# Encoder layer on one core: the distance table moved ahead of the input, and two half-norms interleaved in one row of steps

## The chip, the cores and the metric

The kernel runs on one core of a Trainium2 chip. The metric is device time in microseconds (us) of one launch; lower is better. The core's engines are TensorE (PE), VectorE (DVE), ScalarE (ACT), GpSimd (POOL) and SyncE (SP, which issues most of the DMAs). Each engine works through its own queue in order; semaphores tie the queues together.

## The reference, cut to what matters

One layer of a hybrid attention encoder over 512 prompt tokens and 64 sample tokens, all in float32:

```python
u = rms_norm(h, g_mix_pre)                       # h: 576 tokens x 1024
qa, ka, va, qb, kb, vb = split(u @ w_in)
lam = exp(sum(lq[0]*lq[1])) - exp(sum(lq[2]*lq[3])) + lam0
oa  = band_attention(qa, ka, va, rel_bias)       # mixer A, 8 heads of 64
s   = qb @ kb.T / 8 - slope[head] * abs(q_pos - k_pos)      # mixer B, ALiBi distance penalty
ob  = rms_norm((softmax(s0) - lam * softmax(s1)) @ vb) * (1 - lam0)
g_a, g_b = sigmoid(u @ w_gate)
mix = (g_a * (oa @ w_branch_a) + g_b * (ob @ w_branch_b)) @ w_out
h = h + rms_norm(mix, g_mix_post)                                       # update 0
f = square(relu(rms_norm(h, g_ffn_pre) @ w_up)) @ w_down
h = h + rms_norm(f, g_ffn_post)                                         # update 1
h = h + sigmoid(h @ w_ple_gate) * rms_norm(p @ w_ple, g_ple)
```

## The kernel before, in words

Activations lie transposed (128 channels of a block k on the partitions, 576 tokens along the free axis); a block k is one of KB = 8. Every large product is made in float32 precision from three passes: weights and activations are split into a high and a low part, and TensorE adds hi*hi, lo*hi and hi*lo. A weight piece of 128x512 is loaded by SP into `w_raw`, its high part is made by ScalarE (`hi_part`, L757), its low part by GpSimd (`lo_part`, L569), and TensorE multiplies it. Tokens are taken in two halves of 288 (h = 0, 1).

**The start.** SP loads x (`x_tm`, L428 to L434). TensorE turns it (L1791), ScalarE makes `act_hi` (`split_x`, L770), VectorE makes `act_lo` and keeps `hT` (L1181, L1184). The first of these need `gcol`, the gains, which VectorE copies at L1176. TensorE then makes the k, q and v of unit 0 (L1816, L1736). VectorE scales them by the row of norms (`projected`: k at L1216, q at L1213, v at L1216 once more, as `projected(Count(0), 2)`, L1249). Between q and v stand, in VectorE's queue: the two lambda products and their sum (L1231 to L1234), the distance table (L1236 to L1244: it waits for GpSimd's iota at L590, casts it to float, takes the absolute value, overwrites a corner and halves it into `tab_b[0]`), a wait for ScalarE's exponential of the lambda sums, and two instructions on it (L1246, L1248). TensorE's next work after the v product is to turn v (`V4`, L1894), so it waits for L1216. Then it computes the first scores (`S 0`, L1859) and three steps of unit 1's projection (L1736, 18 matmuls) before the next scores. GpSimd halves the table for the next head at L654, behind its weight splits.

**The updates.** After the output product, and again after the last down product, the layer adds a normalised block sum to `hT`. This is `update(n, ...)`, n = 0 or 1, in VectorE's queue, with partners of the same step order in three other queues. For each block k and half h:

- `normed_half(k, h)` (L1459) multiplies the block by gain and norm row, which TensorE has put into `score` (`half_row`, L2039, announced by `row_ready`). For k in 2, 5, 7 VectorE also adds the block to `hT` (L1464); for the others GpSimd does (L716).
- ScalarE (`split_hi`, L961 or L963, then L965) makes `act_hi` of the new block and puts a copy of the block into the one PSUM place `h_stage`. It refills `h_stage` only when VectorE has read the one before.
- `rest(k, h)` (L1470 for n = 0, L1475 for n = 1) makes `act_lo` from `h_stage` and posts `h_split`.
- TensorE (`behind_norm`, L2076, products at L2048) multiplies two output blocks by block k of half h when `h_split` says so, first all k of half 0, then all of half 1.

VectorE runs `normed_half` two blocks ahead of `rest` within a half: all of half 0 with its eight rests, then a wait for the second `row_ready`, then half 1, which begins with three `normed_half` and the add of block 2 before its first rest.

Of the kernel before, what the change touches and what calls it, by code (L numbers as in the profile page):

```python
# [28 lines left out]
ALU, ACT, AX = mybir.AluOpType, mybir.ActivationFunctionType, mybir.AxisListType  # L29
# [4 lines left out]
MASK = -1e30  # L34
# [68 lines left out]
def at_least(eng, sem, count):  # L103

    v = count.value()
    assert not count.terms or count.const > 0
    if not isinstance(v, int) or v > 0:
        eng.wait_ge(sem, v)
# [9 lines left out]
def encoder_layer(nc, x_prompt, x_sample, cache_a_k, cache_a_v, cache_b_k, cache_b_v, p_prompt, p_sample,  # L118
# [4 lines left out]
    SMP = x_sample.shape[1]  # L123
# [3 lines left out]
    KB = D // P  # L127
# [7 lines left out]
    TW = SEQ + P  # L135
# [37 lines left out]
    CHAIN = (0, 2, 3, 5)  # L173
# [12 lines left out]
    with ExitStack() as ctx:  # L186
        def sb(name, shape, dt=F32, stack=ctx):
            return stack.enter_context(nc.sbuf_tensor(name, shape, dt))

        def sem(name):  # L190
            return ctx.enter_context(nc.semaphore(name))
# [26 lines left out]
        with ExitStack() as band_only:  # L218
            sb("oa_hi_first", [P, T], F32, band_only)
            tab_b = [sb(f"tab_b{b}", [P, TW], F32, band_only) for b in range(2)]  # L220
# [3 lines left out]
        with ExitStack() as branch_a:  # L224
            oa_hi, oa_lo = sb("oa_hi", [P, NA, T], F32R, branch_a), sb("oa_lo", [P, NA, T], F32R, branch_a)

            with ExitStack() as att:
# [12 lines left out]
                with ExitStack() as early:  # L240
                    dist_i, dist = sb("dist_i", [P, TW], I32, early), sb("dist", [P, TW], F32, early)
# [87 lines left out]
        consts, dist_made = sem("consts"), sem("dist_made")  # L329
# [10 lines left out]
        tab_ready = sem("tab_ready")  # L340
# [19 lines left out]
        row_ready, row_read = sem("row_ready"), sem("row_read")  # L360
# [21 lines left out]
        def tokens(h):  # L382
            return slice(HALF * h, HALF * h + HALF)

        def last_square(n, k, h):

            return SQUARES[n] + KB - 2 + 2 * h + k - (KB - 2)
# [753 lines left out]
        def _(dve):  # L1141
            own = [Count(0)]

            def done(ins):

                ins.then_inc(vec, 1)
                own[0] = own[0] + 1

            def settle():

                at_least(dve, vec, own[0])
# [17 lines left out]
            for b in range(2):  # L1169
# [2 lines left out]
                dve.memset(o_tm[b][SMP:P, QB - 1], 0.0)  # L1172
                dve.memset(o_ms[SMP:P, b, QB - 1:QB], 0.0)

            dve.wait_ge(rows_turned, 1)
            dve.tensor_copy(gcol[:, 0:8], proj[0][:, 0:8]).then_inc(gains_ready, 1)  # L1176

            for i, (j, h) in enumerate(X_TILES):
# [3 lines left out]
                                         in1=act_hi[:, j, c].bitcast(F32), op0=ALU.mult, op1=ALU.subtract  # L1182
# [44 lines left out]
            for n in range(2):  # L1227
# [5 lines left out]
            settle()  # L1233
            dve.tensor_reduce(lam_s[:, 0:2], lam_pr[:, :, :], AX.X, ALU.add).then_inc(lam_ready, 1)  # L1234

            dve.wait_ge(dist_made, 1)  # L1236
            done(dve.tensor_copy(dist[:, :], dist_i[:, :]))
            settle()
            done(dve.scalar_tensor_tensor(out=tab_b[0][:, :], in0=dist[:, :], scalar=-1.0, in1=dist[:, :],
                                          op0=ALU.mult, op1=ALU.max))  # L1240
            settle()
            done(dve.memset(tab_b[0][0:SMP, TW - SMP:TW], -2e2 * MASK))
            settle()
            dve.tensor_scalar(tab_b[0][:, :], tab_b[0][:, :], -0.5, None, ALU.mult).then_inc(tab_ready, 1)  # L1244
            dve.wait_ge(lam_exped, 1)
            done(dve.tensor_tensor(lam_s[:, 0:1], lam_s[:, 3:4], lam_s[:, 2:3], ALU.subtract))  # L1246
            settle()
# [165 lines left out]
            with dve.Fori(0, KB // 2) as it:  # L1413
                for j in range(2):
                    n = Count(j, [(it, 2)])
# [10 lines left out]
            def add_square(n, first=False, cols=slice(0, T)):  # L1426

                dve.wait_ge(squared, n + 1)
                if first:
                    dve.tensor_copy(sq_sum[:, cols], sq[n % 2][:, cols]).then_inc(sq_added, 1)  # L1430
                else:
                    dve.wait_ge(sq_added, n)
                    dve.tensor_tensor(sq_sum[:, cols], sq_sum[:, cols], sq[n % 2][:, cols], ALU.add
                                      ).then_inc(sq_added, 1)
# [7 lines left out]
            def means(n, h):  # L1442

                dve.wait_ge(sum_turned, CHAIN[n] + h + 1)
                c = slice(3 * h, 3 * h + 3)
                dve.tensor_scalar(ms_t[0:THIRD, c], turn[0:THIRD, c], 1.0 / D, EPS, ALU.mult, ALU.add
                                  ).then_inc(ms_ready, 1)
# [6 lines left out]
            def update(n, x, g, keep):  # L1454


                def normed_half(k, h):
                    c = tokens(h)
                    dve.scalar_tensor_tensor(out=x[:, k, c], in0=x[:, k, c], scalar=gcol[:, g + k:g + k + 1],  # L1459
                                             in1=score[:, 512 * h:512 * h + HALF], op0=ALU.mult, op1=ALU.mult  # L1460
                                             ).then_inc(block_normed, 1)
                    if k in BY_VECTOR:
                        dve.wait_ge(block_normed, (2 * n + h) * KB + k + 1)
                        dve.tensor_tensor(hT[:, k, c], hT[:, k, c], x[:, k, c], ALU.add).then_inc(h_added[1], 1)  # L1464

                def rest(k, h):
                    c = tokens(h)
                    dve.wait_ge(h_hi, (2 * n + h) * KB + k + 1)
                    if n == 0:
                        dve.scalar_tensor_tensor(out=act_lo[:, k, c], in0=h_stage,  # L1470
                                                 scalar=gcol[:, G_FPRE + k:G_FPRE + k + 1],
                                                 in1=act_hi[:, k, c].bitcast(F32), op0=ALU.mult, op1=ALU.subtract
                                                     ).then_inc(h_split, 1)
                    else:
                        dve.tensor_tensor(act_lo[:, k, c], h_stage, act_hi[:, k, c].bitcast(F32), ALU.subtract  # L1475
                                          ).then_inc(h_split, 1)

                for k in range(KB - 2, KB):
                    keep(k, 0)
                for k in range(KB - 2, KB):  # L1480
                    add_square(last_square(2 * n, k, 0), cols=tokens(0))
                means(2 * n, 0)
                keep(KB - 2, 1)
                add_square(last_square(2 * n, KB - 2, 1), cols=tokens(1))
                dve.wait_ge(row_ready, CHAIN[2 * n] + 1)
                normed_half(0, 0)
                normed_half(1, 0)
                keep(KB - 1, 1)
                add_square(last_square(2 * n, KB - 1, 1), cols=tokens(1))
                for k in range(2, KB):  # L1490
                    normed_half(k, 0)
                    rest(k - 2, 0)
                    if k == 2:
                        means(2 * n, 1)
                rest(KB - 2, 0)
                rest(KB - 1, 0)
                dve.wait_ge(row_ready, CHAIN[2 * n] + 2)
                for k in range(KB):
                    normed_half(k, 1)
                    if k >= 2:  # L1500
                        rest(k - 2, 1)
                rest(KB - 2, 1)
                rest(KB - 1, 1)

            for m in range(KB - 2):
                b = (PJ_OUT + m) % 2
# [723 lines left out]
```

## Time and profile before

| what | value |
|---|---|
| three runs | 1117.22, 1113.8, 1116.96 us; median 1116.96 us |
| the profiled execution's own time | 1117.23 us |
| its span in the trace | 1115.6 us |
| TensorE busy | 1091.6 us (98%) |
| VectorE, ScalarE, GpSimd busy | 52%, 47%, 47% |
| mean granted TensorE clock | 0.994 of full |

The profiled execution has 1.6 us outside its span. Shares are averages over the whole span. The granted clock has two levels, 1.0 (2.4 GHz) and 0.5 (1.2 GHz).

### The profile page before, as it was taken

To read this page: it belongs to the slowest core of one execution; us is meant where nothing else is said; L and a number is where in the kernel's file an instruction comes from. 1 tells how busy PE (TensorE), PEld (TensorE's weight loads), DVE (VectorE), ACT (ScalarE), POOL (GpSimd) and SP (SyncE) were. 2 spreads that over 40 slices of the span, in tenths; PEclk is the share of its full clock that TensorE was granted. 3 is DMA by queue.
4 is the path that set the end of the run, shared out by engine and by line. 5 is a ranking of instruction groups with operands and counts; after the bars stand their busy time and mean duration, and the time that the engine had idled before them with its cause. 6 is when DMAs were issued, how large, how long until landed. Compare 5 with 4: busy or idle time off the path is not lost.

```text
span 1115.6 us, 22618 instructions
## 1 busy us (share of the span) xinstructions
PE 1091.6 (98%) x8252; PEld 1049.1 (94%) x8252; DVE 583.7 (52%) x1192; ACT 521.3 (47%) x1119; POOL 526.7 (47%) x432
## 2 busy tenths in 40 slices
PE   8899999999999999999999999999999999999897
PEld 7899999999889889999999989999999999999897
DVE  5656766666656641112442564878316613833755
ACT  6355455555555553331233467346424722743652
POOL 3556555565455424343445544454444444443651
PEclk9899999999999999999999999999999999999999
DMA  8234434343243322232222213232322322322123
GB/s 185 67 88 105 106 93 100 100 117 88 61 105 98 98 70 85 81 100 79 81 85 79 73 53 90 80 86 82 104 85 77 115 76 75 105 86 76 57 77 85
DMA packets 219618, 99.14 MB, mean 89 GB/s; under 512 B 62786, under 2 KB 216635, under 8 KB 219539
## 3 DMA queue, kind: packets, MB, share of 16 engines
q1 hardware_dynamic: 214098, 88.74, 29.8%
q0 software_dynamic: 5440, 9.34, 2.6%
q8 instruction: 50, 0.82, 0.3%
q14 instruction: 30, 0.24, 0.1%
HBM read 88.57 MB, written 11.02 MB: 89 GB/s over the span
## 4 chain that ended last, share of the span: by engine, by line
PE 90%; DVE 5%; ACT 2%; issue 1%; DMA 1%; SPq 0%; ACTq 0%; DVEq 0%
PE proj L1736 62%; PE proj L2135 12%; PE score L1859 3%; PE proj L2048 2%; PE turn_out L1919 2%; PE turn_out L1949 2%; PE turn_out L1941 1%; PE turn_out L1946 1%; PE score L1871 1%; PE proj L2009 1%; DMA x_tm<-x_sample 1%; PE turn_out L1894 1%; ACT turn_out L965 1%; DVE hT L1464 0%; DVE act_lo L1470 0%
## 5 line engine op out<-in xcount | busy, mean ns | idle before, releaser
L569 POOL TENSOR_TENSOR w_lo<-w_raw,w_hi 128x512 fp32r<-128x512 f32 x292 | 389.7, 1341 | 468.8 <-ACT w_hi L757 468.2
L757 ACT ACTIVATE w_hi<-w_raw 128x512 fp32r<-128x512 f32 x292 | 181.8, 628 | 303.2 <-PE proj L1736 259.6
L1736 PE MATMUL proj<-act_hi,w_hi 128*128 128x288 f32 x1088 | 246.5, 308 | 0.7 <-ACT wide L1124 0.3
L1736 PE MATMUL proj<-act_lo,w_hi 128*128 128x288 f32 x1088 | 233.6, 296 | 0.0
L1736 PE MATMUL proj<-act_hi,w_lo 128*128 128x288 f32 x1088 | 233.1, 296 | 0.0
L1736 PEld LDWEIGHTS proj<-act_hi,w_hi 128*128 128x128 f32 x1088 | 172.6, 190 | 12.5 <-issue 7.4
L1736 PEld LDWEIGHTS proj<-act_hi,w_lo 128*128 128x128 f32 x1088 | 175.6, 189 | 0.0
L1736 PEld LDWEIGHTS proj<-act_lo,w_hi 128*128 128x128 f32 x1088 | 175.4, 189 | 0.0
L1736 PE MATMUL proj<-mid_hi,w_hi 128*128 128x288 f32 x608 | 130.5, 295 | 0.0
L1736 PE MATMUL proj<-mid_lo,w_hi 128*128 128x288 f32 x608 | 130.4, 295 | 0.0
L1736 PE MATMUL proj<-mid_hi,w_lo 128*128 128x288 f32 x608 | 130.3, 295 | 0.0
L1736 PEld LDWEIGHTS proj<-mid_hi,w_hi 128*128 128x128 f32 x608 | 97.5, 188 | 0.0
L1736 PEld LDWEIGHTS proj<-mid_hi,w_lo 128*128 128x128 f32 x608 | 97.4, 188 | 0.0
L1736 PEld LDWEIGHTS proj<-mid_lo,w_hi 128*128 128x128 f32 x608 | 97.3, 188 | 0.0
L820 ACT ACTIVATE prob<-prob,neg_max 128x128 f32<-128x128 f32 (+4 forms) x108 | 62.5, 580 | 66.1 <-DVE neg_max L1265 65.8
L1265 DVE CUSTOM_DVE_ANT_0 prob<-score,tab_b 128x128 f32<-128x128 f32 (+4 forms) x80 | 40.9, 539 | 35.8 <-PE score L1859 19.4
L1559 DVE TENSOR_TENSOR wide<-proj,wide 128x576 f32<-128x576 f32 x24 | 18.1, 754 | 73.7 <-PE proj L1736 73.7
L846 ACT ACTIVATE probT<-turn_out 128x512 f32<-128x512 f32 (+3 forms) x88 | 38.0, 431 | 36.5 <-PE turn_out L1919 22.9
L1384 DVE TENSOR_TENSOR wide<-proj,x_row 128x576 f32 (+1 forms) x13 | 9.9, 758 | 73.9 <-PE proj L1736 73.9
L1919 PE MATMUL turn_out<-ident,prob 128*128 128x128 f32 x208 | 36.3, 278 | 0.5 <-DVE mid_lo L1365 0.4
L2048 PE MATMUL proj<-act_hi,w_hi 128*128 128x288 f32 x96 | 30.9, 322 | 4.9 <-DVE act_lo L1475 2.1
L1265 DVE CUSTOM_DVE_ANT_0 prob<-score,tab_a 128x128 f32<-128x128 f32 (+4 forms) x40 | 20.4, 541 | 18.5 <-PE score L1859 13.4
(312 smaller groups left out, 2106.9 us busy)
## 6 DMA issues: line engine op xcount, KB each, us to landing
w_raw<-w_in SPq DMA_DIRECT2D x72, 256.0 KB, 3.3
w_raw<-w_up SPq DMA_DIRECT2D x64, 256.0 KB, 2.9
w_raw<-w_down SPq DMA_DIRECT2D x64, 256.0 KB, 2.8
w_raw<-w_gate SPq DMA_DIRECT2D x32, 256.0 KB, 2.8
w_raw<-w_branch_b SPq DMA_DIRECT2D x16, 256.0 KB, 2.7
w_raw<-w_out SPq DMA_DIRECT2D x16, 256.0 KB, 2.8
w_raw<-w_ple_gate SPq DMA_DIRECT2D x16, 256.0 KB, 2.8
out<-k_out SPq DMA_DIRECT2D x48, 64.0 KB, 1.9
```

The costliest lines, as they stand in the source:

```text
L569: pool.tensor_tensor(w_lo[:, slot], w_raw[:, slot], w_hi[:, slot].bitcast(F32), ALU.subtract).then_inc(lo_done, 1)
L757: act.activation(w_hi[:, slot], w_raw[:, slot], ACT.Copy).then_inc(hi_done, 1)
L820: act.activation(prob[b][m][0:np_, 0:n], prob[b][m][0:np_, 0:n], ACT.Exp, scale=-1.0, bias=neg_max[0:np_, b, m:m + 1], accum_out=sums[0:np ...
L846: act.activation(probT[m][0:np_, 0:n], turn[0:np_, 0:n], ACT.Copy).then_inc(turn_free, 1)
L1265: last = dve.tensor_tensor_reduce(prob[b][m][rs, 0:n], score[rs, 512 * m:512 * m + n], tab, -1.0, 3e38, ALU.add, ALU.min, neg_max[rs, b, m ...
L1559: dve.tensor_tensor(halves(d), acc[b], halves(d), ALU.add).then_inc(proj_free[b], 1)
L1736: last = pe.matmul(out[:, h], w[:, slot, at], x[:, k, HALF * h:HALF * h + HALF], start=(k == 0 and s == 0), stop=(k == blocks - 1 and s == 2))
L1859: last = pe.matmul(score[:, 512 * m:512 * m + n], q[par][h, P * i:P * i + P], k[par][h, 0:n], start=(s == 0), stop=(s == 2))
L1919: last = pe.transpose(turn[:, P * j:P * j + P], prob[i % 2][0 if i == QB - 1 else m][:, P * j:P * j + P], ident[:, :])
L1949: last = pe.matmul(outp[:, 0:P], probT[0][:, P * j:P * j + P], v_tm[:, j, :], start=(j == 0), stop=(j == i))
L2048: last = pe.matmul(acc[n % 2][:, h], w[:, slot, at], x[:, k, tokens(h)], start=(k == 0 and s == 0), stop=(k == KB - 1 and s == 2))
L2135: last = pe.matmul(bank, a[:, at], b[:, k0 + k, cols], start=(k == 0 and s == 0), stop=(k == KB // 2 - 1 and s == 2))
```

## The change

Two edits, both in VectorE's queue. The number and kind of instructions stay the same. The four instructions of the distance table and their wait go from behind the lambda sums to behind the first memsets, ahead of the copy of the gains. In `update`, the two loops over half 0 and half 1 become one loop of 16 steps in which `normed_half` runs two steps ahead of `rest` across the border of the halves, with the wait for the second norm row ahead of step 8.

```diff
                 dve.memset(o_ms[SMP:P, b, QB - 1:QB], 0.0)
 
+            dve.wait_ge(dist_made, 1)
+            done(dve.tensor_copy(dist[:, :], dist_i[:, :]))
+            settle()
+            done(dve.scalar_tensor_tensor(out=tab_b[0][:, :], in0=dist[:, :], scalar=-1.0, in1=dist[:, :],
+                                          op0=ALU.mult, op1=ALU.max))
+            settle()
+            done(dve.memset(tab_b[0][0:SMP, TW - SMP:TW], -2e2 * MASK))
+            settle()
+            dve.tensor_scalar(tab_b[0][:, :], tab_b[0][:, :], -0.5, None, ALU.mult).then_inc(tab_ready, 1)
+
             dve.wait_ge(rows_turned, 1)
             dve.tensor_copy(gcol[:, 0:8], proj[0][:, 0:8]).then_inc(gains_ready, 1)
...
             dve.tensor_reduce(lam_s[:, 0:2], lam_pr[:, :, :], AX.X, ALU.add).then_inc(lam_ready, 1)
 
-            dve.wait_ge(dist_made, 1)
-            done(dve.tensor_copy(dist[:, :], dist_i[:, :]))
...
-            dve.tensor_scalar(tab_b[0][:, :], tab_b[0][:, :], -0.5, None, ALU.mult).then_inc(tab_ready, 1)
             dve.wait_ge(lam_exped, 1)
...
-                for k in range(2, KB):
-                    normed_half(k, 0)
-                    rest(k - 2, 0)
-                    if k == 2:
+                for step in range(2, 2 * KB + 2):
+                    if step == KB:
+                        dve.wait_ge(row_ready, CHAIN[2 * n] + 2)
+                    if step < 2 * KB:
+                        normed_half(step % KB, step // KB)
+                    rest((step - 2) % KB, (step - 2) // KB)
+                    if step == 2:
                         means(2 * n, 1)
-                rest(KB - 2, 0)
-                rest(KB - 1, 0)
-                dve.wait_ge(row_ready, CHAIN[2 * n] + 2)
-                for k in range(KB):
-                    normed_half(k, 1)
-                    if k >= 2:
-                        rest(k - 2, 1)
-                rest(KB - 2, 1)
-                rest(KB - 1, 1)
```

## Rows read from the trace of the kernel before

**Rows 1.** The page: chain that ended last, shares by engine.

```profile
PE 90%; DVE 5%; ACT 2%; issue 1%; DMA 1%; SPq 0%; ACTq 0%; DVEq 0%
```

**Rows 2.** Waits of PE: line waited for: total us, times, longest.

```profile
PE turn_out L1894 <- DVE vT L1216: 2.8, 1, 2.8
```

**Rows 3.** Timeline of VectorE, 34 to 42 us: start, length, what [idle before].

```profile
34.59 1.42 DVE L1237 CAST dist<-dist_i 128x640 f32<-128x640 int32 x1
36.05 1.80 DVE L1239 SCALAR_TENSOR_TENSOR tab_b<-dist 128x640 f32<-128x640 f32 x1
...
39.26 1.21 DVE L1246 TENSOR_TENSOR lam_s<-lam_s 128x1 f32<-128x1 f32 x1
...
40.58 0.75 DVE L1216 TENSOR_TENSOR vT<-proj,x_row 128x576 f32<-128x576 f32 x1
```

**Rows 4.** Timeline of PE: last matmuls ahead of the wait for v.

```profile
38.29 0.43 PE L1736 MATMUL proj<-act_lo,w_hi 128*128 128x288 f32 x2
```

**Rows 5.** Chain in order of time, units 0 and 1: start, length, what.

```profile
41.47 1.09 PE turn_out L1894 x4
42.56 0.83 PE score L1859 x5
43.39 4.62 PE proj L1736 x18
...
73.79 0.59 PE turn_out L1894 x4
74.38 0.48 PE score L1859 x6
74.86 2.57 PE proj L1736 x18
```

**Rows 6.** Windows: busy us by engine, then granted PE clock, DMA share, GB/s.

```profile
45.00:46.00 1.00, 1.00 (x6) 1.00 (x6) 0.96 (x3) 0.00 (x0) 0.00 (x0) 0.50 0.00 0
...
649.00:650.00 1.00, 1.00 (x6) 1.00 (x6) 0.96 (x3) 0.87 (x3) 0.57 (x1) 0.50 0.00 0
```

**Rows 7.** Timeline of GpSimd, 34 to 44 us.

```profile
34.24 1.43 POOL L605 TENSOR_TENSOR q_lo<-q_raw,q_hi 128x576 fp32r<-128x576 f32 x1
35.62 1.54 POOL L569 TENSOR_TENSOR w_lo<-w_raw,w_hi 128x512 fp32r<-128x512 f32 x1
...
41.66 1.82 POOL L654 TENSOR_SCALAR tab_b<-tab_b 128x640 f32<-128x640 f32 x1
```

**Rows 8.** Timeline of the start: GpSimd, VectorE and ScalarE.

```profile
1.42 0.66 POOL L590 IOTA dist_i<- 128x640 int32 x1
...
5.88 0.17 DVE L1176 COPY gcol<-proj 128x8 f32<-128x8 f32 x1 [2.94 <-PE proj L1784]
...
8.65 0.89 ACT L770 ACTIVATE act_hi<-score,gcol 128x288 fp32r<-128x288 f32 x2 [0.59 <-PE score L1791]
```

**Rows 9.** Timeline of VectorE, update 1, border of the halves.

```profile
1050.32 0.46 DVE L1475 TENSOR_TENSOR act_lo<-turn_out,act_hi 128x288 fp32r<-128x288 f32 x1 [0.48 <-ACT turn_out L965]
1051.26 0.46 DVE L1475 TENSOR_TENSOR act_lo<-turn_out,act_hi 128x288 fp32r<-128x288 f32 x1 [0.48 <-ACT turn_out L965]
1051.63 1.36 DVE L1459 SCALAR_TENSOR_TENSOR wide<-wide,gcol,score 128x288 f32<-128x288 f32 x3
1053.02 1.06 DVE L1464 TENSOR_TENSOR hT<-hT,wide 128x288 f32<-128x288 f32 x1
1054.01 0.45 DVE L1475 TENSOR_TENSOR act_lo<-turn_out,act_hi 128x288 fp32r<-128x288 f32 x1
...
1056.79 0.46 DVE L1464 TENSOR_TENSOR hT<-hT,wide 128x288 f32<-128x288 f32 x1
```

**Rows 10.** Timeline of PE: norm row and first product of half 1, both updates.

```profile
647.32 0.41 PE L2048 MATMUL proj<-act_hi,w_hi 128*128 128x288 f32 x1 [1.75 <-DVE act_lo L1470]
...
1043.45 0.80 PE L2039 MATMUL score<-ident,r_t 96*128 96x96 f32 x6
...
1054.51 0.40 PE L2048 MATMUL proj<-act_hi,w_hi 128*128 128x288 f32 x1 [1.68 <-DVE act_lo L1475]
```

**Rows 11.** GpSimd's adds in the updates: count, min/median/max ns, first and last start.

```profile
L716 POOL TENSOR_TENSOR hT<-hT,wide x20: 785/805/810, 628.9 to 1058.1; 128x288 f32<-128x288 f32 x20
```

More of the change, by code:

```diff
@@ L1234, in _ @@
             dve.tensor_reduce(lam_s[:, 0:2], lam_pr[:, :, :], AX.X, ALU.add).then_inc(lam_ready, 1)
-            dve.wait_ge(dist_made, 1)
-            done(dve.tensor_copy(dist[:, :], dist_i[:, :]))
[L1238 to L1243, printed above, removed]
-            dve.tensor_scalar(tab_b[0][:, :], tab_b[0][:, :], -0.5, None, ALU.mult).then_inc(tab_ready, 1)
             dve.wait_ge(lam_exped, 1)
```

## The prediction

> **What bounds the kernel now.** I read the page's chain first: 90% of it is TensorE's own work [rows 1], so the change can only pay where TensorE stands still or runs slowly. The waits of TensorE come next. The longest single one in the list is the turning of the first v, behind VectorE's L1216: 2.8 us, once [rows 2]. Two more of 1.75 and 1.68 us stand where the products of half 1 begin in the two updates [rows 10]. The change touches exactly these three places. The windows add what the list of waits hides: after the first wait TensorE runs at a granted clock of 0.50, the 1.2 GHz level [rows 6].
>
> **Part A, the table, taken off the path.** TensorE's last v matmuls end at 38.29 + 0.43 = 38.72 [rows 4]. L1216 could start then, but starts at 40.58 because VectorE is still in the table (34.59 to about 39.3) and then in L1246, which lasts to 40.47 [rows 3]. Without the table, L1246 is reached at about 34.6 plus ScalarE's small exponential. It is drawn out by GpSimd: the cast beginning at 34.59 ended at 36.01, 0.34 us after GpSimd's q_lo ended at 35.67, and L1239 ended at 37.85, 0.69 after the split that ended at 37.16 [rows 3, 7]. So L1246 may stand until one GpSimd instruction ends (about 36 to 37), still well before 38.72. Then L1216 starts with the end of the matmuls, about 38.76 (the trace's usual hand-over is a few hundredths), lasts 0.75, and TensorE begins 0.14 after its end, as before (41.33 to 41.47) [rows 3, 5]. That is 39.65 instead of 41.47: 1.82 us. What is late next is v itself, so a wait of 0.93 us stays.
>
> **Part A, the clock.** From 41.47, four transposes, the first scores and 18 matmuls take 1.09 + 0.83 + 4.62 = 6.54 us at the lower level [rows 5, 6]. The same three pieces in unit 1, with no wait ahead of them, take 0.59 + 0.48 + 2.57 = 3.64 [rows 5]. What TensorE did before the clock fell was to stand still for 2.75 us (38.72 to 41.47). If the 0.93 us that stay don't bring the clock down, 2.90 us more are saved; if they do, nothing of it. So the term lies between 0 and 2.90. I take 2.90. The nearest rows are the two of about 1.7 us: the one before 647.32 was followed by 0.50 some 1.7 us later, the one before 1054.51 left the matmul behind it at its usual 0.40 [rows 6, 10]. Waits of 1.7 us are thus the borderline of this trace and 0.93 is about half of them.
>
> **Part A, where the table goes.** VectorE is idle from 2.94 to 5.88, waiting for TensorE's turned gains [rows 8]. The iota it needs has ended at 2.08, so the new wait does not hold. Behind it stand only the gain copy and its users; ScalarE first uses the gains at 8.65 [rows 8]. The price of the table with GpSimd in the way is 34.59 to about 39.3, 4.7 us, so it ends at 7.7 at worst, and the copy of 0.17 is done before 8.65. Without GpSimd, which has no arithmetic there, cast and absolute value cost 0.34 and 0.69 plus some hundredths each, and the halving is taken like the cast, one input and as many elements: an estimate of 1.5 to 2 us, inside the 2.94 that are idle. Either way the cost is nothing. If that cover were gone, each further microsecond would shift the whole start.
>
> This placement has one rule against it. The Trainium skill, page "SBUF — State Buffer" (the "DVE blocks DMA" trap), says that VectorE instructions which take both read ports, fp32 copies among them, keep GpSimd from writing the descriptors of DMAs it issues, so that such DMAs starve. By that rule the x loads would suffer if GpSimd issued them; they stand in SP's queue, so by the rule the sum stays as it is. No run here shows a load issued by GpSimd beside such a copy.
>
> **Part A, what comes next.** At full clock the second scores are due at 39.65 + 3.64 = 43.29. They need VectorE's two bias instructions on the first scores, and in the trace these came only when GpSimd's halving (41.66 to 43.48) was over [rows 7]. That halving stands behind four splits which the table held up: by 0.34 and 0.69 for its first two instructions, about 1.4 us in all. It now ends between 42.1 and 43.5. The pair then takes at most 0.9, by two of the normed halves of 0.45 that have over twice as many columns [rows 9]. So it is done between 42.6 (at half of that) and 44.4, and a new wait of 0 to 1.1 us may appear here. I take 0, since most of the 1.4 us should come back.
>
> **Part B, the row of 16.** In update 1 the rests of blocks 6 and 7 of half 0 begin at 1050.32 and 1051.26, each after 0.48 us in which VectorE waits for ScalarE's stage [rows 9]. Only behind them come three normed halves (1051.63, 1.36 for the three), the add of block 2 (1.06, at 1053.02) and the first rest of half 1 at 1054.01; TensorE, which had waited 1.68, goes on at 1054.51 [rows 9, 10]. In the new order the first two normed halves go ahead of those two rests. One costs some 0.45 to 0.5, so each fits the 0.48 in which VectorE stood. The second norm row that they wait for has been there since 1043.45 + 0.80 = 1044.25 [rows 10], over 5 us earlier; nothing queued behind the moved wait is held.
>
> After the rest of block 7 (done 1051.7) there remains one normed half and the add. The add took 1.06 because GpSimd was in its own adds, of 0.8 us each [rows 11]. Now GpSimd gets its first two blocks at about 1050.3 and 1051.2 and is done near 1052.0, so the add of VectorE should take the 0.46 that it takes alone [rows 9]; 1.06 is the upper bound. The sum: 1051.63 + 0.46 for one normed half (1.36/3), + 0.46 for the add = 1052.55 for the first rest, against 1054.01: 1.46 us sooner. ScalarE has the stage filled by then: it must wait for the rest of block 7 at 1051.7, and VectorE never stood longer than 0.48 for it in the rows of that border.
>
> TensorE's half 0 ended 1.68 before 1054.51, at 1052.83; its first product of half 1 then starts at 1053.05. From there half 1 runs at the pace of the rests, as before, since that chain (stage, rest, stage) is unchanged: all eight shift by 1.46, and so does TensorE's end. With the add at 1.06 the gain is 0.86; the upper bound is the whole wait, 1.68. In update 0 the rows repeat 407 us earlier, with the wait of 1.75 before 647.32 [rows 10]; the gain there is again 1.46. The lower clock there (649 to 650) [rows 6] costs nothing now, as the rests and not TensorE's speed set the end of that half; a smaller wait can only make it rarer. Part B: 2 x 1.46 = 2.92, bounds 1.7 to 3.4. Work after both updates is TensorE's own again, so it shifts as a whole.
>
> **Sum.** 1.82 + 2.90 + 2.92 = 7.64 us off the profiled 1117.23 gives 1109.6. That execution lies 0.27 above the median of 1116.96. The run at 1113.8 is 3.4 lower than the other two, near the 2.9 that the low clock costs: some executions of the kernel before may escape it.
>
> **The rivals.**
> - *The clock falls all the same.* The remaining 0.93 us, followed by transposes and small scores, is enough. For it: one 1.75 us wait did bring the clock down. Against: it is half as long. Then 1.82 + 2.92 = 4.74: 1112.5.
> - *The row of 16 pays little.* The add and the stage of half 1 collide with GpSimd and ScalarE, and the first rest comes hardly sooner, since ScalarE's single stage is the real pace. For it: every rest of half 0 waited for ScalarE [rows 9]. Against: between 1051.7 and 1054.0 it was VectorE that was busy throughout. Gain 4.72 from part A alone: 1112.5.
> - *The table does not free v.* L1246 is held behind GpSimd's back-to-back splits up to the point where v would have been late anyway, and the clock falls too. For it: its 1.21 us for one column [rows 3]. Against: four us of slack. With part B only: 1114.3.
> - *Slower: the early table holds up the start.* Place: VectorE from 2.94, ahead of the gain copy. Price: one us for each us by which the copy ends after 8.65, as ScalarE's first split and all of x stand behind it. It decides only if the table takes over 5.5 us, and with the gains of the sum the kernel gets slower than before only beyond 5.5 + 7.6 = 13.1 us. For it: the x loads, ScalarE and TensorE are all at work there, and no row shows the table beside them. Against: 4.7 us was the price even in GpSimd's way [rows 3]. At three times that, 14.1 us, the copy ends 8.6 late: 1118.2.
>
> **How the numbers follow.** Forecast 0.70, clock falls 0.12, row pays little 0.09, v not freed 0.05, slower 0.04. The forecast's own range is 1109.1 to 1111.9 (part B's bounds and the new wait of up to 1.1). The range for 8 in 10 goes up past the 1112.5 of two rivals to 1113.0; below the own range it leaves 1.0 us, twice what remains of the spread of the three runs (3.4 us) when the 2.9 of the low clock are taken off: 1108.1 to 1113.0. About 0.3%, 3.4 us, can be told from no change, that is a time under 1113.6: forecast and the first two rivals, 0.91, less some for a median of before that falls near 1113.8: faster 0.86, same 0.10, slower 0.04.
>
> **What would show it.** Right: the four table instructions between 2.9 and 5.9, together about 2 us; TensorE's wait before L1894 near 0.9 us; a granted clock of 1.0 from 41 to 48; the wait before half 1 down from 1.7 to a few tenths in both updates. Wrong: 0.50 in the windows after 40 us, a gain copy later than 5.9, a wait of TensorE for the bias at 43 to 45 us of over half a microsecond, or VectorE's add of block 2 still near 1 us at the border of the halves.

## The result and the profile after

The changed kernel takes 1111.07 us (median of 9 runs, 1109.44 to 1111.75), against 1117.22 for the kernel before beside it (9 runs, 1113.80 to 1121.14): a ratio of 0.9939, with a 95% interval of 0.9928 to 0.9951. That is 6.15 us less, or 0.55%, more than the 0.3% that can be told from no change. By means it is 1117.23 - 1110.68 = 6.55 us. The forecast was 1109.6. The profiled execution took 1109.61, 7.62 less than the profiled one of before (1117.23). One execution among those of the experiments below, of 1735.2 us with a mean granted clock of 0.556 over its whole length (the table-only kernel), is left out of the ratios and means.

In the page's chain TensorE's share rises from 90% to 93% and VectorE's falls [rows 1]:

```profile
PE 93%; DVE 4%; ACT 2%; issue 1%; DMA 1%; SPq 0%; ACTq 0%; DVEq 0%
```

The waits of PE (line waited for: total us, times, longest). The wait for v [rows 2] is down to a third, and the two of 1.7 us in the updates are no longer among the long ones. Those that stay were there before, apart from a second wait for x and the short ones at the borders (two longer lines ahead of these, of 2.7 and 1.9 us in all, are the same in both):

```profile
...
PE turn_out L1950 <- DVE o_tm L1360: 1.6, 1, 1.6
PE turn_out L2025 <- DVE sq_sum L1434: 1.3, 2, 0.6
PE score L1786 <- DMA x_tm<-x_prompt: 1.1, 2, 0.7
PE proj L2043 <- DVE act_lo L1471: 1.1, 4, 0.3
PE turn_out L1889 <- DVE vT L1226: 0.9, 1, 0.9
```

The timeline of VectorE at the start (start, length, what, and in brackets the idle time before; the memset of the corner, 0.11, is left out). The whole table stands where VectorE was idle [rows 8] and is done at 5.02; the gain copy starts at 5.58, as soon as TensorE has the gains:

```profile
2.95 0.49 DVE L1176 CAST dist<-dist_i 128x640 f32<-128x640 int32 x1
3.48 0.82 DVE L1178 SCALAR_TENSOR_TENSOR tab_b<-dist 128x640 f32<-128x640 f32 x1
...
4.52 0.50 DVE L1183 TENSOR_SCALAR tab_b<-tab_b 128x640 f32<-128x640 f32 x1
5.58 0.17 DVE L1186 COPY gcol<-proj 128x8 f32<-128x8 f32 x1 [0.56 <-PE proj L1779]
```

The same timeline at the place that the table left [rows 3]. VectorE now stands ready 2.87 us before TensorE's v product ends; TensorE then waits only for the scaling of v itself. The pair on the first scores' bias comes at 42.70:

```profile
33.03 0.76 DVE L1223 SCALAR_TENSOR_TENSOR q_raw<-proj,x_row 128x576 f32<-128x576 f32 x1
...
35.89 0.74 DVE L1247 TENSOR_TENSOR lam_s<-lam_s 128x1 f32<-128x1 f32 x1 [0.27 <-ACT lam_s L808]
...
39.69 0.76 DVE L1226 TENSOR_TENSOR vT<-proj,x_row 128x576 f32<-128x576 f32 x1 [2.87 <-PE proj L1731]
...
42.70 0.29 DVE L1266 CUSTOM_DVE_ANT_0 prob<-score,tab_b 128x128 f32<-128x128 f32 x1
```

GpSimd beside it [rows 7]. Its four splits take 5.16 us in one row (6.05 before), and its halving runs while VectorE's pair is at work:

```profile
36.57 5.16 POOL L569 TENSOR_TENSOR w_lo<-w_raw,w_hi 128x512 fp32r<-128x512 f32 x4
41.70 1.83 POOL L654 TENSOR_SCALAR tab_b<-tab_b 128x640 f32<-128x640 f32 x1
```

The chain in order of time (start, length, what): unit 0 now goes through its first scores at the lengths of unit 1 [rows 5]:

```profile
40.59 0.63 PE turn_out L1889 x4
41.22 0.48 PE score L1854 x5
41.70 2.59 PE proj L1731 x18
44.29 0.55 PE score L1854 x6
```

The windows (busy us of PE, PEld, DVE, ACT, POOL; then the granted clock, the DMA share, GB/s). 0.50 is gone at both places of [rows 6]. It stands at a new place, 8.4 to 15.4 us, while x loads and the first products run on it:

```profile
9.00:11.00 2.00, 1.93 (x16) 1.58 (x14) 2.00 (x5) 2.00 (x5) 1.04 (x1) 0.50 1.04 275
...
42.00:44.00 2.00, 2.00 (x17) 2.00 (x16) 1.22 (x7) 0.88 (x4) 1.52 (x1) 1.00 0.71 206
44.00:46.00 2.00, 2.00 (x18) 1.71 (x17) 1.93 (x8) 0.59 (x2) 0.00 (x0) 1.00 0.16 46
...
648.00:650.00 2.00, 1.79 (x12) 1.51 (x12) 0.52 (x1) 1.24 (x4) 2.00 (x2) 1.00 0.00 0
```

VectorE at the border of the halves in update 1 [rows 9]. There is no idle time in brackets left; behind the last rest of half 0 (1045.12) stand one normed half and an add of 0.46, and then the first rest of half 1:

```profile
1045.12 0.46 DVE L1476 TENSOR_TENSOR act_lo<-turn_out,act_hi 128x288 fp32r<-128x288 f32 x1
1045.50 0.51 DVE L1460 SCALAR_TENSOR_TENSOR wide<-wide,gcol,score 128x288 f32<-128x288 f32 x1
1046.04 0.46 DVE L1465 TENSOR_TENSOR hT<-hT,wide 128x288 f32<-128x288 f32 x1
1046.42 0.45 DVE L1476 TENSOR_TENSOR act_lo<-turn_out,act_hi 128x288 fp32r<-128x288 f32 x1
```

TensorE at the two borders, and its second norm row, done at 1038.13, some 5 us ahead of VectorE's first normed half of half 1 [rows 10]:

```profile
641.17 0.40 PE L2043 MATMUL proj<-act_hi,w_hi 128*128 128x288 f32 x1 [0.29 <-DVE act_lo L1471]
...
1037.32 0.81 PE L2034 MATMUL score<-ident,r_t 96*128 96x96 f32 x6
...
1046.92 0.40 PE L2043 MATMUL proj<-act_hi,w_hi 128*128 128x288 f32 x1 [0.22 <-DVE act_lo L1476]
```

### The profile page after: what moved, and what is told of

The parts are those of the page before. It is cut to its first block, busy times and chain, and to the rows that moved or that the text cites. A ratio compares the mean times of both kernels' runs of the same rounds, so it can differ in the third digit from the quotient of the medians.

```text
span 1108.0 us, 22618 instructions
## 1 busy us (share of the span) xinstructions
PE 1090.1 (98%) x8252; PEld 1047.3 (95%) x8252; DVE 578.3 (52%) x1192; ACT 521.5 (47%) x1119; POOL 526.3 (47%) x432
## 4 chain that ended last, share of the span: by engine, by line
PE 93%; DVE 4%; ACT 2%; issue 1%; DMA 1%; SPq 0%; ACTq 0%; DVEq 0%
PE proj L1731 63%; PE proj L2130 12%; PE score L1854 3%; PE proj L2043 2%; PE turn_out L1914 2%; PE turn_out L1944 2%; PE turn_out L1936 1%; PE turn_out L1941 1%; PE score L1866 1%; PE proj L2004 1%; PE proj L1811 1%; PE turn_out L1889 1%; ACT turn_out L965 1%; DMA x_tm<-x_prompt 1%; DVE act_lo L1471 0%
```

## The experiments

Every kernel was timed beside the kernel before, in three comparisons of four kernels, each on one chip; across comparisons, only differences to the kernel before are like for like. The theory: four separate gains, 1.82 (wait for v), 2.90 (the clock behind it) and twice 1.46 (the borders). The rivals: that the parts are not separate, that the early table costs something while x loads, and, when the median came out 1.5 above the forecast, two accounts of where the changed kernel still loses time in some of its executions.

**One part alone: the table.** The kernel before with the first two hunks of the change (the table's lines moved ahead of the gain copy) and the old order in the updates.

> The kernel before with the table moved ahead of the gain copy, the updates as they were. Theory (wait and clock): TensorE's wait ahead of the first turned v falls from 2.75 to about 0.93 us (1.82), and the granted clock stays at 1.0 from 41 to 48 us (2.9 more): 4.7 us off, a ratio near 0.996, and the waits of about 1.7 us at the border of the halves stay. Rival (the clock falls all the same): only 1.8 us off, ratio 0.998, and 0.50 again behind the wait. Rival (all of the gain sits in the updates): no gain, ratio 1.000.

Measured: 1113.6 against 1117.29, ratio 0.9973 (0.9961 to 0.9985). The expected 0.996 lies just outside the interval, and the 0.998 of the rival "the clock falls all the same" lies inside it, so the time does not decide between them; the profile does. The granted clock is 1.00 in every window from 39 to 49 us, where the rival has 0.50, and the four transposes of v take 0.63 us. Why the gain is smaller than 4.7 on the average follows from the experiment on the clock below. Timeline of TensorE: the wait for v is 0.94, both waits of the borders are untouched:

```profile
41.60 0.63 PE L1895 MATMUL turn_out<-ident,vT 128*128 128x128 f32 x4 [0.94 <-DVE vT L1226]
...
643.70 0.40 PE L2049 MATMUL proj<-act_hi,w_hi 128*128 128x288 f32 x1 [1.74 <-DVE act_lo L1471]
...
1050.95 0.40 PE L2049 MATMUL proj<-act_hi,w_hi 128*128 128x288 f32 x1 [1.69 <-DVE act_lo L1476]
```

**The other part alone: the row of 16.** The kernel before with the last hunk only.

> The kernel before with the row of 16 steps, the table left where it was. Theory: the waits of 1.75 and 1.68 us at the border of the halves fall to 0.2 to 0.3, 1.46 us in each update, 2.9 us off, ratio near 0.9974; the wait of 2.75 us ahead of the first v and the low clock behind it stay as they were. Rival (ScalarE's one stage is the pace): under 1 us off in all.

Measured: 1114.38, ratio 0.9977 (0.9962 to 0.9991), with the expected 0.9974 inside. The wait for v stays, with the clock mostly at 0.50 behind it (0.57 in the window), and the long waits of both borders are gone (the longest left is 0.3 in the list of waits); the border of update 1:

```profile
43.19 1.01 PE L1888 MATMUL turn_out<-ident,vT 128*128 128x128 f32 x4 [2.76 <-DVE vT L1216]
...
1052.07 0.40 PE L2042 MATMUL proj<-act_hi,w_hi 128*128 128x288 f32 x1 [0.23 <-DVE act_lo L1475]
```
```profile
45.00:47.00 2.00, 2.00 (x11) 2.00 (x10) 1.00 (x7) 0.88 (x4) 0.20 (x1) 0.57 0.37 110
```

The parts are separate. By means, the table alone saves 1116.55 - 1113.30 = 3.25 and the row alone 1116.55 - 1113.94 = 2.61, together 5.86; both together save 6.55 in the comparison of the result and 5.95 in the second one (1116.69 - 1110.74). This profile also has a stretch at 0.50 while x loads (9.2 to 16 us), with the table at its old place, so the early table is not needed for that. Whether it makes that fall more frequent is open: it stands in the profile of one of the three kernels with the table at its old place, and in five of the nine with the early table and the narrow idle products at the start.

**The clock by itself.** The kernel before, v as late as ever, but TensorE busy until then:

```diff
+            pe.wait_ge(proj_free[1], 1)
+            keep_warm(10, 512)
             unit(Count(0), "B", 0, None)
```

> The kernel before with ten idle matmuls (128x512, nobody reads their output) put between the v product and the turning of v: TensorE works while it waits, and v comes no sooner. Theory (the standstill brings the clock down): granted clock 1.0 from 41 to 48 us, the turning still begins near 41.5, and 2.9 us are gained, ratio near 0.9974. Rival (the clock falls for another reason, or transposes and small scores bring it down): 0.50 behind it as before, no gain, ratio 1.000.

Measured: 1114.48 (1112.9 to 1115.7), ratio 0.9985 (0.9973 to 0.9998): the 1.000 of the rival is excluded, and the expected 0.9974 is at the edge. By means the kernel gains 1116.55 - 1114.50 = 2.05 us. The ten idle products lie in the wait, v is turned at the old distance from the products ahead of it, and the clock stays up:

```profile
38.23 2.47 PE L1770 MATMUL proj<-idle_x,idle_w 128*128 128x512 f32 x10
41.09 0.66 PE L1896 MATMUL turn_out<-ident,vT 128*128 128x128 f32 x4 [0.39 <-DVE vT L1216]
```
```profile
42.00:44.00 2.00, 2.00 (x20) 1.93 (x17) 1.20 (x8) 1.27 (x5) 1.21 (x1) 1.00 0.64 184
```

So the low clock behind the wait costs time by itself, some 3 us, but not in every execution. The 29 executions of the kernel before in this comparison fall into two groups: 11 with a mean granted clock of 0.996 or more, 1113.3 to 1115.5 (mean 1114.4), and 18 below it, 1115.9 to 1119.1 (mean 1117.9). The kernel that was kept busy has the times of the lower group alone (mean 1114.5). The clock therefore fell behind the wait in about 18 of 29 executions of before (inferred from the two groups; in the other two comparisons 14 of 22 executions of before have a clock below 0.996), and the term is worth an estimated 2.9 x 0.62 = 1.8 on the average, beside the 2.05 of this experiment; with the wait, 1.82 + 1.8 = 3.6 for the table, against 3.25 measured by means and 3.7 by medians.

**The rest of the wait for v.** The changed kernel, TensorE's order in unit 0 alone:

```diff
+                order = list(walk(steps, prev == "B"))
+                if prev is None:
+                    order = [order[1], order[2], order[0]] + order[3:]
-                for name, arg, t in walk(steps, prev == "B"):
+                for name, arg, t in order:
```

> The changed kernel, and in unit 0 TensorE computes the first scores and one step of unit 1's projection before it turns v. Theory (0.93 us of waiting for v are left): the work of 0.48 + 0.86 us fits into that wait, the second scores come 0.9 us sooner, and the kernel is 0.9 us below the changed one, 8.5 us below before in the profiled sum. Rival (VectorE's bias pair behind GpSimd's halving is late next): the wait moves to the second scores, gain under 0.3 us.

Measured: 1108.84 (1107.92 to 1111.13), ratio 0.9938 (0.9921 to 0.9956). The wait for v is gone, and 0.23 us of waiting for the bias pair have come at the second scores, under the 0.3 of the rival. The 8.5 below the kernel before are met by the medians (8.45); by means it is 7.2, 0.65 to 1.25 more than the two comparisons give the changed kernel, so the size of this gain is not settled. In this profile the clock fell somewhere else, right behind the wait for the normed output of unit 7, 1.5 to 1.6 us in every kernel that keeps the order there:

```profile
291.33 0.63 PE L1953 MATMUL turn_out<-ident,o_tm 128*128 128x128 f32 x4 [1.57 <-DVE o_tm L1360]
```
```profile
292.00:296.00 4.00, 3.78 (x20) 2.46 (x19) 2.11 (x6) 1.86 (x4) 1.28 (x1) 0.60 0.05 12
296.00:298.00 2.00, 2.00 (x11) 2.00 (x10) 0.55 (x4) 1.88 (x5) 0.00 (x0) 0.50 0.00 0
```

**Where the changed kernel loses 1.5 us in some executions.** First the kernel unchanged, in a new comparison.

> The changed kernel again, in the same comparison as the next three, to see where its executions lose the clock. In its first executions four of nine ran at a mean granted clock of 0.997 to 1.0 and 1109.4 to 1110.3 us, five at 0.996 and 1111.1 to 1111.8. Theory A (the clock that falls in the slower ones falls behind the 1.57 us wait for the normed output at L1950, some 250 us behind the place that the change cured): the same two groups, and a profile out of the slower one shows a stretch at 0.50 at about 291 to 298. Theory B (it falls while x loads, as in the profile at hand, 8.6 to 15.4): the same two groups, and a profile of the slower one has its 0.50 only in the first 20 us.

Measured: 1110.83 (1108.74 to 1111.87), ratio 0.9943 (0.9923 to 0.9963). Both theories missed half of it: as they have it, three executions at 0.996 took 1110.5 to 1110.9, but two at 0.999 and 1.0 took 1111.7 and 1111.9. The profiled one (1111.65, clock 0.999) has no 0.50 ahead of its last few us and shows what else can cost time: TensorE waits 1.25 and 1.08 us for the scores' bias in the middle of two units of mixer A, which the profile of the change has nowhere. In the timelines, VectorE's normalisation of a 128x256 tile (0.35 when nothing is beside it) lasts 3.92, from the moment at which GpSimd's split of the cache keys begins to just behind the third of its splits in a row, which end at 358.05 + 2.52 = 360.57:

```profile
356.80 3.92 DVE L1321 TENSOR_SCALAR prob<-prob,r_sum 128x256 f32<-128x256 f32 x1
```
```profile
356.80 1.28 POOL L639 TENSOR_TENSOR ckT_lo<-ckT,ckT_hi 128x512 fp32r<-128x512 f32 x1
358.05 2.52 POOL L569 TENSOR_TENSOR w_lo<-w_raw,w_hi 128x512 fp32r<-128x512 f32 x2
```
```profile
362.68 0.51 PE L1854 MATMUL score<-k_hi,q_hi 64*128 64x512 f32 x2 [1.08 <-DVE neg_max L1266]
```

The profile of the change has a shorter case, behind which TensorE doesn't wait: VectorE's instruction lasts 2.67 there and ends at 358.26, just behind the second of the three splits (356.85 + 1.26 = 358.11):

```profile
355.59 2.67 DVE L1321 TENSOR_SCALAR prob<-prob,r_sum 128x256 f32<-128x256 f32 x1
```

The kernel before had the long case too, in the profile on which the prediction rests:

```profile
359.40 3.93 DVE L1320 TENSOR_SCALAR prob<-prob,r_sum 128x256 f32<-128x256 f32 x1
```
```profile
365.29 0.50 PE L1859 MATMUL score<-k_hi,q_hi 64*128 64x512 f32 x2 [0.97 <-DVE neg_max L1265]
```

**The wait for the normed output.** The changed kernel, with two k steps and the first attention product ahead of that turn, in unit 8 on TensorE alone:

```diff
+                if kind == "A" and prev == "B":
+                    ot = next(n for n, o in enumerate(order) if o[0] == "OT")
+                    later = next(n for n in range(ot + 3, len(order)) if order[n][0] == "k")
+                    order = (order[:ot] + order[ot + 1:ot + 3] + [order[later], order[ot]]
+                             + order[ot + 3:later] + order[later + 1:])
```

> The changed kernel with another order on TensorE alone in the first unit of the second kind (unit 8): two k steps and the first attention product ahead of the turn of the normed output, which waits 1.57 us today. Both theories: the wait at that turn goes to under 0.3, and with it some 1.3 to 1.6 us of every execution. Theory A: the executions at 0.996 go too (those left are at 0.997 or above), so the median falls by 1.5 plus some 1 to 1.6, to about 1108.2 to 1108.6, and the spread of the executions narrows to under 1.2. Theory B: the two groups stay, 1.6 us apart, each about 1.5 lower, median 1109.5.

Measured: 1109.67 (1107.74 to 1110.66), ratio 0.9931 (0.9912 to 0.9951), 1.2 less than the changed kernel in this comparison, with six executions each, spread over some 3 us. Neither theory foresaw that the wait only moves, to the next turn, which needs the bank that VectorE has to empty of the normed output:

```profile
PE turn_out L1920 <- DVE mid_lo L1366: 1.6, 1, 1.6
```

The next turn waited 0.40 in the changed kernel, so of 1.57 + 0.40 some 0.4 is saved. Executions at 0.996 remain (2 of 6), and the profile of one of them has its 0.50 from 8 to 15.5 us and then only in the last few us, as every profile here: theory B for this one.

**Both orders.** The last kernel and the order of unit 0 from above.

> The last kernel's order in unit 8, and in the first unit the first scores and one k step ahead of the turn of V (which alone had given 1108.84, with executions from 1107.9 to 1111.1). Both theories: 0.9 less than the kernel with the order in unit 8 alone, no wait ahead of the turn of V. Theory A: about 1107.3 to 1107.6, all executions within 1.2. Theory B: about 1108.0, in two groups.

Measured: 1109.02 (1108.34 to 1110.81), ratio 0.9933 (0.9913 to 0.9952): between the orders of unit 0 alone and of unit 8 alone, no sum. Against the order of unit 8 alone it is 0.65 less where 0.9 was expected. The order of unit 8 is worth nothing that these runs can show.

**The sums of the second half one product later.** Added to the last kernel:

```diff
                 project_ple(half, 0)
-                half_sums(n, 1)
                 project_ple(half, 1)
+                half_sums(n, 1)
```

> The last kernel, and behind the MLP's norms the sums of the second half one product later (behind the second of the per-layer products rather than the first), where TensorE waits 0.62 us for VectorE's squares twice. Both waits under 0.1, 1.2 us less than the kernel before it: 1106.1 to 1106.8. A rival: the row of the second half then comes too late, and the updates of half 1 (that the change moved to VectorE ahead of it) wait on it: no gain, or a new wait of 0.3 to 0.8 ahead of the first gate product of half 1.

Measured: 1108.43 (1106.66 to 1110.03), ratio 0.9921 (0.9902 to 0.9941). The two waits of 0.62 for the squares are gone from the list; 0.36 for a weight split came in place of one of them. The expected 1106.1 to 1106.8 is missed. It is 0.6 less in the median than the kernel without it, about as large as what is left of the waits (1.24 - 0.36 = 0.9), and not to be told from it with six executions each.

**The collision of VectorE and GpSimd.** The changed kernel; GpSimd finishes the next unit's table behind the third split of the unit (k step 11) rather than at its start, where it waits over 3 us for the table's DMA:

```diff
                     if name == "k" and arg % 4 == 3:
                         lo_part((u + 1) * 6 + (arg // 4 + RING))
+                        if arg == 11 and table is not None:
+                            finish_table(table)
...
-                    finish_table(a + 1)
```

> The changed kernel with the GpSimd copies that finish the next unit's table (0.82 and 0.23 us) put behind the third weight split of the unit rather than at its start, where they wait 3.1 to 3.8 us for the table's DMA and hold the splits of the cache keys and of two weights back into one row of three. Theory C (VectorE's L1321 at 128x256, 0.35 us when free, is held for as long as GpSimd works without a pause, 2.67 to 3.93 us, when it starts with that row, and TensorE then waits 0.9 to 1.3 us at the scores of the fourth block): no L1321 over 2 us and no wait of TensorE for neg_max over 0.3, and 0.5 to 1.5 us off the median, 1109.5 to 1110.3, with the slowest executions gone. Rival (VectorE's length comes from its own operands, and the row of GpSimd is beside it by chance): L1321 keeps its cases of 2.7 to 3.9 us and the median stays at 1110.8 to 1111.1.

Measured: 1108.46 (1107.78 to 1108.88), ratio 0.9922 (0.9907 to 0.9937). What theory C expected is there. The splits no longer stand in one row of three, and VectorE's normalisation (count, min/median/max ns, first and last start, forms) has no case over 1.6 us, that of the 576-column tile, where most of the kernels above had 2.7 to 3.9; the list of waits has none for neg_max:

```profile
319.99 1.27 POOL L641 TENSOR_TENSOR ckT_lo<-ckT,ckT_hi 128x512 fp32r<-128x512 f32 x1 [1.06 <-ACT ckT_hi L855]
321.23 1.29 POOL L569 TENSOR_TENSOR w_lo<-w_raw,w_hi 128x512 fp32r<-128x512 f32 x1
325.52 1.29 POOL L569 TENSOR_TENSOR w_lo<-w_raw,w_hi 128x512 fp32r<-128x512 f32 x1 [3.00 <-ACT w_hi L757]
```
```profile
L1321 DVE TENSOR_SCALAR prob<-prob,r_sum x36: 285/421/1590, 285.4 to 401.5; 128x128 f32<-128x128 f32 x8, 128x256 f32<-128x256 f32 x8, 128x384 f32<-128x384 f32 x8, 128x512 f32<-128x512 f32 x8
```

One profile without a case proves little by itself: the kernel with the first scores ahead of the turn of V has the row of three (from 326.25) and no case either, since VectorE's instruction was through at 326.13. But of the eleven profiles with the table finished at the start of the unit, ten have a case of 2.7 to 3.9, and none of the three with the later finish has one. Where the case lasts 3.9 TensorE waits 0.9 to 1.3 behind it, where it lasts 2.7 it doesn't.

The gain, 2.4 against the changed kernel of the comparison before, is more than the 0.5 to 1.5 expected; the changed kernel itself was not timed in this comparison, and the two intervals overlap. Part of it may be that one execution of six had a clock under 0.997 here, and three there; why that is so, these runs don't tell.

**The start.** The changed kernel; the idle products between the arrivals of x four times as wide:

```diff
                 if c < 2:
-                    keep_warm(2, P)
+                    keep_warm(2, 512)
```

> The changed kernel with the two idle products between the arrivals of x 512 columns wide instead of 128, so that TensorE's waits for x (0.40 and 0.68 us in the profile with the clock at 0.50 from 8.6 to 15.4) shrink to under 0.4. Theory B (the slower group of the changed kernel's executions loses its clock while x loads): no execution at a mean granted clock of 0.996, q_raw at 31.8 to 32.1 rather than 33.0, median 1109.8 to 1110.2. Rival (that fall comes from something other than those waits): two groups as before, median 1110.8 to 1111.1, or later by up to 0.4 where the wider idle products hold up the turns of x.

Measured: 1109.83 (1109.32 to 1112.06), ratio 0.9934 (0.9919 to 0.9949). No execution at 0.996 or below (0.997 to 0.999) and a median in the range of theory B; but the profiled one, the slowest, still has a fall, behind TensorE's wait of 1.47 us ahead of its first product (10.1 to 11.6), with q_raw at 33.10 and not the expected 31.8 to 32.1, and two collisions. That wait of 1.47 stands in six other profiles without a fall:

```profile
11.00:13.00 2.00, 1.39 (x6) 1.43 (x7) 1.52 (x4) 2.00 (x5) 1.74 (x2) 0.69 1.05 242
```

**Three and four moves together.** The changed kernel with the order of unit 0, the later sums and the later finish of the table; then the wider idle products as well.

> The changed kernel with the first scores ahead of the turn of V in unit 0 (0.9 us), the later finish of the table (0.5 to 1.5 in the executions that have the collision) and the sums of the second half one product later (0.9, by the wait of 0.36 that took the place of the 0.62 twice in the last kernel of the batch before). 1107.5 to 1108.3 for the median.

> The last kernel and the wider idle products while x loads. Theory B: 0.5 to 1.2 us less than the last, 1106.6 to 1107.5, with executions within 1.5 of one another. Rival: the same as the last.

Measured: 1107.99 (1106.06 to 1108.81), ratio 0.9913 (0.9897 to 0.9930), and 1106.88 (1106.61 to 1107.26), ratio 0.9908 (0.9893 to 0.9923), both as expected. The first has two groups, three executions at 0.999 (mean 1106.8) and three at 0.996 (mean 1108.5); its profile, of the second group, has its 0.50 while x loads. The second has one group, 0.65 us wide, and its profile has no stretch at 0.50 ahead of the last few us. This version takes 10.3 less than the kernel before beside it, and some 4 less than the changed kernel took in the other comparisons.

## Why the prediction was right

- **The wait for v, 1.82 of it.** Right to the hundredth: 2.75 to 0.94. From q_raw to the turn of v, 9.38 us became 7.56. The reason was right too, with L1247 at 0.74 through by 36.7, 3 us ahead of the products' end.
- **The clock, 2.90 between 0 and 2.90.** Right in mechanism and in this execution: 0.94 us of standing still was followed by 1.00, and the three pieces take 0.63 + 0.48 + 2.59 = 3.70 against 6.54, 2.84 saved. On the average it is mis-sized: the prediction saw that some executions of before may escape, but took the term whole, and it is paid in about 18 of 29 (2.05 on the average by the idle products). The argument from a "borderline" at 1.7 us does not hold up: the clock fell behind a wait of 1.57 and stayed up behind one of 1.73 in these runs.
- **The table at the start at nothing.** 2.07 us (2.95 to 5.02), hardly over the estimate of 1.5 to 2; the gain copy starts 0.3 earlier than before and ScalarE's first split at 8.46 rather than 8.65. Nothing behind the table was held up. The start of this execution was late all the same, q_raw at 33.03 rather than 32.09, with the lower clock from 8.4 to 15.4: the seven profiles without such a fall have q_raw at 31.76 to 32.75, the seven with one at 33.03 to 34.04. The profile with the row alone, and the table at its old place, is one of the latter.
- **The new wait for the bias, 0 between 0 and 1.1.** Zero, but the reading behind it was wrong. The pair came at 42.70, before the halving was over and not behind it; the second scores were due at 43.29 + 0.94 and came at 44.22. In the kernel the pair waits for the scores alone. The profile of before names the halving only because it ended last (43.48); the scores had ended at 42.56 + 0.83 = 43.39, late by the lower clock, and the pair followed:

```profile
43.55 0.29 DVE L1265 CUSTOM_DVE_ANT_0 prob<-score,tab_b 128x128 f32<-128x128 f32 x1 [0.71 <-POOL tab_b L654]
```

  After the change the scores end at 41.70, and what stands ahead of the pair is VectorE's own four casts of q behind v (40.37 to 42.67). Of the 1.4 us that the table was thought to cost GpSimd's splits 0.89 came back, but nothing hung on it.
- **Part B, 1.46 per update between 0.86 and 1.68.** 1.75 to 0.29 and 1.68 to 0.22: 1.46 each. The add of block 2 took 0.46, as taken; the first two normed halves fit the gaps of 0.48. The rival's ground, that every rest of half 0 waited for ScalarE, was misread: in update 1 four of the eight did.
- **The sum.** +0.94 (the later start) - 1.82 - 2.84 - 0.96 (the collision at 359 us that the profile of before had, with a wait of 0.97 behind it; the profile after had only the short case without a wait) - 1.47 - 1.45 = -7.60, against 7.64 predicted and 7.62 between the two profiles. So the two profiled times agree in part by luck: two chance terms of 0.9 cancelled.
- **The median.** 1111.07, not 1109.6. Four of nine executions stand near the forecast (1109.4 to 1110.3), five at 1111.1 to 1111.8 with a clock of 0.996. Counted at its share, the clock term fits the means: 1.82 + 1.8 + 2.92 = 6.5 against 6.55 and 5.95. It does not explain the median, for the execution of before at the median (1117.22) is the profiled one, which pays. The 1.5 lies in the slower executions of the changed kernel, and none of those five was profiled. Profiles of others show falls of the clock while x loads and the collisions of VectorE and GpSimd; the fall alone isn't enough, since the profiled execution has it and took 1109.61. So which of them makes up the 1.5 is not shown. Neither is new: the profile of before has the collision, and the row alone, with the table at its old place, has the fall.
- **The rivals.** "The clock falls all the same", "the row pays little", "the table doesn't free v" and "the early table holds up the start" are each refuted by the row above that answers to them, the last as far as the gain copy and ScalarE's first split go; whether the early table makes the fall of the clock at the start more frequent stays open.

The collision fits what the Trainium skill states (page "SBUF — State Buffer", section "SBUF: two separate sides"): VectorE, in some of its instructions, and GpSimd share a pair of ports that whichever starts first holds for its whole instruction, while the other stands still. The trace agrees, and shows more: in the cases of 3.92 VectorE did not get in between GpSimd's instructions, but stood for all three of a row, and in the case of 2.67 for two of the three. That it is these ports is not shown by a run of its own.

## What to carry to other kernels

A stall of TensorE can have two prices: its own length, and the lower clock behind it (2.75 and 2.84 us here). Read the second from the windows, and count it by the share of executions that pay it, which the times and clocks of many executions tell and one profile cannot. Moving a VectorE stage into a place where its engine is idle and GpSimd has no arithmetic shortened it as well (4.7 us to 2.07 here), and interleaving two independent rows filled the gaps of 0.48 in which the engine waited for a stage of another. When two profiles differ by the sum that was predicted, check landmark by landmark that it is made of the terms that were predicted.

## What the runs showed that was not expected

- A VectorE instruction of 0.35 us stood for 2.67 to 3.93 us behind two or three GpSimd instructions without a pause between them. Whether it meets them differs from profile to profile; the row starts when the DMA of the table has landed (waits of 3.1 to 3.8 us), so the landing is the likely cause. With the row taken apart the six executions agree within 1.1 us.
- The clock fell behind waits of 2.75, 1.75, 1.68 and 1.57 us, and not behind others of the same length: the border of update 1 waits 1.68 in the profile of before and in that of the kernel kept busy, and only the second has 0.50 behind it (1052 to 1055 us); a wait of 1.5 to 1.6 at the turn of the normed output stands in every profile here but the three that moved it, and only one has 0.50 behind it.
- In unit 8 an order that hid one wait of 1.57 us made another of 1.6 at the next turn: the wait belonged to the bank that VectorE had yet to empty, not to the instruction that showed it.
